# Routing one-hots laid out in pairs of tokens, so that every two-byte operand steps by one

## The reference, cut to what matters

```python
u = exp_u[ec]                                       # the picked rows
a = jax.nn.gelu(jnp.einsum('cd,chkd->chk', xc, u))
w = gc * a                                          # gc: gate of each pick
return jnp.einsum('chk,chkd->cd', w, exp_v[ec])
```

## Time and profile before

| | |
|---|---|
| median of 3 runs | 3306.38 us (3305.8 to 3314.76) |
| the profiled execution's own time | 3306.54 us |
| its span | 3304.8 us |
| TensorE's mean granted clock | 0.981 |
| DVE busy | 2340.2 us, 71% |
| PE busy | 3179.6 us, 96% |

### The profile page before, as it was taken

How to read it: one execution, slowest core, us unless ns; L and a number is a source line. 1 busy time by engine, 2 the same in 40 slices (tenths; PEclk the granted TensorE clock), 3 DMA queues, 4 the chain that set the end, 5 groups by cost and what they waited for, 6 DMA issues and landing times.

```text
span 3304.8 us, 71646 instructions
## 1 busy us (share of the span) xinstructions
PE 3179.6 (96%) x31390; PEld 2836.8 (86%) x31390; DVE 2340.2 (71%) x2685; ACT 1256.1 (38%) x1135; POOL 388.2 (12%) x284
## 2 busy tenths in 40 slices
PE   7999999999999989988989999999999999999998
PEld 4777768899999979988879998888888888888887
DVE  8596145799999877777779877578667766555554
ACT  2010143445444434333434444444443444443332
POOL 0276000000011222232212000200000000000000
PEclk8999999999999989999999999999999999999999
DMA  9657795546678988888788875556555566565553
GB/s 411 250 224 294 291 387 213 171 179 242 202 269 305 342 327 316 314 335 311 293 287 315 317 262 196 198 197 203 191 197 199 173 209 202 198 201 201 202 202 116
DMA packets 105301, 821.57 MB, mean 249 GB/s; under 512 B 12394, under 2 KB 14458, under 8 KB 15552
## 3 DMA queue, kind: packets, MB, share of 16 engines
q1 hardware_dynamic: 86112, 700.49, 58.4%
q0 software_dynamic: 16656, 115.53, 9.1%
q10 hardware_dynamic: 2304, 2.10, 0.2%
HBM read 814.00 MB, written 4.06 MB: 248 GB/s over the span
## 4 chain that ended last, share of the span: by engine, by line
PE 67%; DVE 17%; DMA 10%; issue 4%; ACT 1%; POOL 0%; ACTq 0%; DVEq 0%; SPq 0%; POOLq 0%
PE psW L587 17%; PE psW L588 17%; PE psW L589 17%; DVE ring L1191 7%; PE psW L585 7%; DMA ring<-wst_dram 4%; DMA arena<-urow_dram,rs 3%; DMA proj<-vrow_dram,rs 3%; DVE arena L1668 1%; PE psM L729 1%; PE psW L729 1%; PE psM L883 1%; PE psM L658 1%; ACT ring L2028 1%; DVE proj L1722 1%
## 5 line engine op out<-in xcount | busy, mean ns | idle before, releaser
L1191 DVE SCALAR_TENSOR_TENSOR ring<-ring 128x2048 f16<-128x2048 f32 x526 | 1200.3, 2294 | 522.8 <-ACT ring L2028 521.2
L2028 ACT ACTIVATE ring<-ring 128x2048 f16<-128x2048 f32 x526 | 1000.8, 1907 | 937.2 <-PE psW L589 776.5
L587 PE MATMUL psW<-h_act,ring 128*128 128x256 f16 (+1 forms) x5040 | 1339.7, 266 | 17.9 <-DVE ring L1191 13.0
L588 PE MATMUL psW<-h_act,ring 128*128 128x256 f16 (+1 forms) x5040 | 1338.8, 266 | 0.0
L589 PE MATMUL psW<-h_act,ring 128*128 128x256 f16 (+1 forms) x5040 | 1338.7, 266 | 0.0
L587 PE MATMUL psW<-arena,ring 128*128 128x208 f16 (+1 forms) x3072 | 800.0, 260 | 10.1 <-DVE ring L1191 5.6
L588 PE MATMUL psW<-arena,ring 128*128 128x208 f16 (+1 forms) x3072 | 799.6, 260 | 0.0
L589 PE MATMUL psW<-arena,ring 128*128 128x208 f16 (+1 forms) x3072 | 799.4, 260 | 0.0
L587 PEld LDWEIGHTS psW<-h_act,ring 128*128 128x128 f16 x5040 | 495.4, 98 | 81.1 <-issue 19.9
L589 PEld LDWEIGHTS psW<-h_act,ring 128*128 128x128 f16 x5040 | 495.6, 98 | 35.0
L588 PEld LDWEIGHTS psW<-h_act,ring 128*128 128x128 f16 x5040 | 495.6, 98 | 34.8
(11 more groups left out here) (405 smaller groups left out, 2584.7 us busy)
## 6 DMA issues: line engine op xcount, KB each, us to landing
ring<-wst_dram SPq DMA_DIRECT2D x522, 1024.0 KB
ring<-wst_dram SPq DMA_DIRECT2D x72, 2048.0 KB, 11.3
proj<-h_rows POOLq DMA_DIRECT2D x6, 1024.0 KB
x_res<-xT_dram POOLq DMA_DIRECT2D x2, 2048.0 KB, 17.5
out_dram<-x_res SPq DMA_DIRECT2D x4, 512.0 KB, 2.9
bias_rows<-proj POOLq DMA_DIRECT2D x1, 1536.0 KB, 21.8
x_res<-cmat_dram POOLq DMA_DIRECT2D x1, 1024.0 KB, 7.5
x_res<-bmat_dram ACTq DMA_DIRECT2D x8, 128.0 KB, 2.7
```

The costliest lines, as they stand in the source:

```text
L587: nc.tensor.matmul(out, whi(s, col, P), xh, start=first, stop=False)
L588: nc.tensor.matmul(out, whi(s, col, P), xl, start=False, stop=False)
L1191: ins = stt(wlo(s, c, n), ring[:, s * UNIT + c:s * UNIT + c + n], WSCALE, whi(s, c, n), ALU.mult, ALU.subtract)
L2028: act(whi(s, p2 * (UNIT // 2), UNIT // 2), ring[:, c], ACT.Copy, scale=WSCALE).then_inc(hi_done, 1)
```

## The change

The one-hots of 16 tokens were laid out token by token: the numbers of a token side by side, so the pick's number and the gate had to be repeated along the innermost dimension (step 0 there). Now two neighbouring tokens share a row of pairs: the innermost dimension has the two tokens (`x`), the number (`e`) stands outside it, and the pair of tokens (`t`) outside that. The picks and gates are then read with an inner step of one, two tokens at a time, repeated over `e`. The number table holds each number twice, so it too is read with a step of one; its one copy (L1636) writes 256 elements instead of 128, and the f16 identity moves in `dyn` to make room. PE reads each token out of the pairs: its 128 stationary and 32 moving elements now lie two elements (4 bytes) apart instead of one. The instructions, their number and order on each engine, their element counts (but for the table's copy), buffers, waits and transfers are the same.

```diff
-        ident16 = dyn[:, 320:384].bitcast(F16)
+        ident16 = dyn[:, 384:448].bitcast(F16)
...
-        iota16 = dyn[:, 256:320].bitcast(F16)
-        hot2 = [buf.bitcast(F16).rearrange("p (t e) -> p t e", t=STEP_T) for buf in (A[:, 13312:14336], J[:, 6144:7168])]
-        first1 = W[:, 1536:1792].bitcast(F16).rearrange("p (t e) -> p t e", t=STEP_T)
-        hot1 = [buf.bitcast(F16).rearrange("p (t r e) -> p t r e", t=STEP_T, r=2)
+        iota16 = dyn[:, 256:384].bitcast(F16).rearrange("p (e x) -> p e x", x=2)
+        hot2 = [buf.bitcast(F16).rearrange("p (t e x) -> p t e x", t=STEP_T // 2, x=2) for buf in (A[:, 13312:14336], J[:, 6144:7168])]
+        first1 = W[:, 1536:1792].bitcast(F16).rearrange("p (t e x) -> p t e x", t=STEP_T // 2, x=2)
+        hot1 = [buf.bitcast(F16).rearrange("p (t r e x) -> p t r e x", t=STEP_T // 2, r=2, x=2)
...
-                        mm = nc.tensor.matmul(psM[:, b, t * QUART_T:(t + 1) * QUART_T], hot2[b][:, t, :], hot1[b][:, t, r, :],
+                        mm = nc.tensor.matmul(psM[:, b, t * QUART_T:(t + 1) * QUART_T], hot2[b][:, t // 2, :, t % 2],
+                                              hot1[b][:, t // 2, r, :, t % 2],
                                               start=(r == 0), stop=(r == 1))
...
-                    D.put(v.tensor_copy(iota16, iota[:, :]))
+                    D.put(v.tensor_copy(iota16, iota[:, :].unsqueeze(2).to_broadcast([P, P, 2])))
...
-                def cols(f, w):
-                    return e16[:, f, ROWS_T + STEP_T * n:ROWS_T + STEP_T * (n + 1)].unsqueeze(2).to_broadcast([P, STEP_T, w])
+                def by_pairs(row, w):
+
+                    return row[:, ROWS_T + STEP_T * n:ROWS_T + STEP_T * (n + 1)].rearrange("p (t x) -> p t x", x=2)\
+                        .unsqueeze(2).to_broadcast([P, STEP_T // 2, w, 2])
+
+                def numbers(first, w):
+
+                    return iota16[:, first:first + w, :].unsqueeze(1).to_broadcast([P, STEP_T // 2, w, 2])
...
-                tt(first1, iota16[:, QUART_T * q:QUART_T * (q + 1)].unsqueeze(1).to_broadcast([P, STEP_T, QUART_T]),
-                   cols(0, QUART_T), ALU.is_equal).then_inc(first1_ready, 1)
-                tt(hot2[b], iota16.unsqueeze(1).to_broadcast([P, STEP_T, P]), cols(1, P), ALU.is_equal).then_inc(hot2_ready, 1)
+                tt(first1, numbers(QUART_T * q, QUART_T), by_pairs(e16[:, 0, :], QUART_T), ALU.is_equal).then_inc(first1_ready, 1)
+                tt(hot2[b], numbers(0, P), by_pairs(e16[:, 1, :], P), ALU.is_equal).then_inc(hot2_ready, 1)
...
-                    gate = g16[:, r, ROWS_T + STEP_T * n:ROWS_T + STEP_T * (n + 1)].unsqueeze(2).to_broadcast([P, STEP_T, QUART_T])
-                    ins = tt(hot1[b][:, :, r, :], first1, gate, ALU.mult)
+                    ins = tt(hot1[b][:, :, r, :, :], first1, by_pairs(g16[:, r, :], QUART_T), ALU.mult)
```

## The result

The changed kernel takes **3275.39 us** (median of 4 runs, 3272.77 to 3277.33) beside 3306.09 us for the kernel before (4 runs, 3305.48 to 3314.76): a ratio of 0.9901, with a 95% interval of 0.9883 to 0.9919. The ratio is formed from all the runs, so it isn't exactly that of the two medians (0.9907). The forecast was 3278 us. Times and ratios leave out runs in a slow state, of which there was one, in experiment 4 (4267 us at a granted clock of 0.715).

The account below looks back on a forecast made before the run. It took DVE to set the pace in u0's end and u1, and mostly a chain of transfers with DVE as a link from v0 on. 3306.5 - 15 - 13 = 3278.5, say 3278 us, range 3252 to 3294.

Parts of the forecast that it names:

- DVE's pairs: DVE's mask operations take two elements at a time, saving 1.89 us a step, 98 us of DVE's 2340 over 52 steps.
- The estimate of 1.92 us for hot2: DVE's 2048-element operation under a rule against single 4-byte words; a step would then save some 0.7 us.
- PE's strided reads: PE's loads of 128 stationary elements 4 bytes apart stay at 96 ns, so they cost 0.
- The rival at 3395 us: PE's strided stationary loads are slow, 95 ns more for each of 1664: slower, spread over 3300 to 3400 us; chance 0.13.
- u0's end and u1: Window 850 to 1022, 15 mask steps: term of 15 us, 12.4 from PE's idle time and 2.6 from the lower clock.
- so PE becomes the bound and its 13.6 us of idle time goes: End of u0 and u1: DVE's work falls from 171.6 to 143.3 us, under PE's 158.5.
- in u1 no wait of PE behind a low part over 1 us: A sign to look for in the changed kernel's profile, along with DVE below PE in u1.
- v0 to v2: 37 mask steps: dots, POOL loads and row weights come earlier; term of 13 us, bounds 0 and 56.
- 10 waits for rows or weights: v0 to v2: each PE wait for V rows or weights shortens by one step's 1.9 us, 19 us in all.
- halving the seven transfer waits: v0 to v2: 7 of 10 waits end at a transfer with DMA engines full around them, so 6.5 us was taken off.
- stay as long as now: Sign that the prediction is wrong in size: PE's waits for V rows go altogether or keep their length.
- The middle is all transfers: Rival: DVE saved, u1 gives 15 us, v0 to v2 nothing, 3291 us; counted in the forecast's own range, no separate chance.

Follow-up runs that it names:

- experiment 4: The changed kernel with each number once in the table, repeated over the two tokens by a step of zero: 3285.47 us, ratio 0.9926.
- experiment 1: The changed kernel's pair layout for PE, but DVE builds it token by token, with repeated operands, a single table and writes at a step of two: 3317.87 us.
- Experiment 7: The changed kernel with the masks of steps 0 and 1 built behind the second low part of their unit in u0's last units: 3268.85 us.
- experiment 11: The changed kernel itself, unaltered, measured a second time in a later group of runs: 3272.70 us, ratio 0.9883.
- experiment 5: The changed kernel with V row loads moved ahead of U row loads in POOL's queue where both are due in the same unit: 3237.55 us.
- 3, small ones alone: The changed kernel with only first1 and hot1 in pairs, hot2 built one element at a time into the same layout: 3293.13 us, ratio 0.9941.
- 2, hot2 alone: The changed kernel with only hot2 in pairs, the 512-element operations built one element at a time into the same layout: 3281.18 us, ratio 0.9911.
- 8, half of hot2 as well: The changed kernel with hot2 built for only 64 of the 128 numbers from step 2 on: 3276.54 us, ratio 0.9897.

## Why the prediction was right, and where it was off

**DVE's pairs: right.** 1220 and 419 ns were the lower bounds taken; 1216 and 414 to 416 were measured. The mask lines fell by 98.8 us (98 predicted). The estimate of 1.92 us for hot2, which I had worked out from the Trainium skill ("Vector Engine (DVE) Microarchitecture Reference", 5.2), did not come true: it runs at 1.216. I had stretched that section: its 1.73 ns stands for one source that hops 4 KiB at every element of a stream of 4-byte words, it lists larger figures too, and it has no row for a word that is read again. In experiments 1 to 4 the inner step decides: each operation paired exactly where all three operands step by one. No run has a step of two in the output alone, so it isn't shown that this by itself would lose the pairing.

**PE's strided reads: right.** The rival at 3395 us needed 17 ns more a load; the row says 1 ns, and experiment 1 says it without DVE's gain beside it. So a distance of 4 bytes alone doesn't explain the f32 load's 191 ns in the earlier trace rows; what does, no run here shows.

**u0's end and u1: right, with its parts off against each other.** 15 us predicted, 13.0 measured from the first mask operation to v0 (12.0 the second time). The forecast took the idle time from 13.6 to 1.2 us and 2.6 us from the lower clock; the idle time went to 4.4, and some 3.9 us came otherwise, which fits the granted clock. DVE fell below PE as forecast. The wait before the first routing step went from 2.9 to 1.1 us (the prediction's 3.1 us is another wait, behind L1740 at the end of u1, and that one went whole). The step that was mis-sized is "so PE becomes the bound and its 13.6 us of idle time goes": the stop at the next unit stayed, at 3.3 us where it was 3.6, against the sign "in u1 no wait of PE behind a low part over 1 us". Reckoned from the first mask operation, its release by DVE came 3.7 us earlier, the saving of two mask steps. But PE came 3.5 us earlier too. Windows of PE around the two stops, first of the kernel before (with columns as above: the stop, the work behind it, the work before the next stop):

```profile
857.00:860.00 3.00, 0.31 (x4) 0.07 (x1) 3.00 (x3) 1.91 (x1) 0.00 (x0) 1.00 0.00 0
860.00:866.00 6.00, 5.80 (x47) 5.28 (x48) 5.93 (x7) 0.00 (x0) 0.00 (x0) 0.72 0.77 272
866.00:871.00 5.00, 5.00 (x82) 5.00 (x80) 4.90 (x7) 2.31 (x2) 0.00 (x0) 1.00 0.24 97
```

and then of the changed one:

```profile
859.00:860.00 1.00, 0.02 (x1) 0.00 (x0) 1.00 (x2) 0.82 (x1) 0.00 (x0) 1.00 0.00 0
860.00:864.50 4.50, 4.40 (x53) 4.41 (x54) 4.47 (x5) 1.09 (x1) 0.00 (x0) 1.00 0.73 246
```

Before, a stop of 3 us was followed by 6 us at a granted clock of 0.72, which is 1.2 GHz for a bit over half of them; 47 matmuls ran. After, a stop of 1 us was followed by 1.00, and 53 matmuls ran in 4.5 us. PE regained 1.7 us there, beside the 1.8 of the shorter stop, and waited for DVE with both at the next stop. Up to the end of that stop DVE sets the pace in both kernels. Experiment 7, which takes the masks out of the way of those low parts, fits the reading: the stop shrinks to 2.5 us.

**v0 to v2: right in sign, low in size, and by another way than I worked out.** 13 us predicted, within bounds of 0 and 56; 17.9 us in the profiled execution (835.1 to 817.2 us), 27.3 in experiment 11's. The step that failed is "10 waits for rows or weights x 1.9". Waits did not each get 1.9 us shorter. The waits that DVE itself ended nearly went (15.9 to 4.3 us), while those for V rows kept most of their sum (40.2 to 38.4 us, and 33.0 in experiment 11's execution) in fewer pieces. The term also had nothing for the clock, though some 4.5 of the 17.9 us came otherwise than through idle time. That halving the seven transfer waits came close in the sum is luck.

**The sum: closer than its parts.** 3278 us stands 3 us from 3275.39. The idle time of PE gave 22.6 us in the windows of the earlier trace rows, not the 25.4 that the two terms hold; the lower clock, at 2.6 in the forecast, makes up for it (some 8 us). By the prediction's own sign its size is wrong if the waits for V rows "stay as long as now"; in the profiled execution they nearly did, and that the time came out all the same is luck as well.

**"The middle is all transfers": half right.** The transfers do hold what is left, and the DMA share there is 0.87 to 0.88. But experiment 5 moves the same bytes in another order and takes the waits away, at a share of 0.90 over the middle. So the place in POOL's queue held them, and a share of 0.87 was no proof of a limit. Nor did I see that the gain saturates. By DVE's busy time against the kernel before (2340.2 us), with the program's time against its own group's:

| | DVE, us | program, us |
|---|---|---|
| 1, distance alone | +8.8 | +8.6 |
| 4, single table | -27.8 | -23.8 |
| 3, small ones alone | -34.0 | -16.1 |
| 2, hot2 alone | -53.3 | -28.1 |
| the change | -93.8 | -30.7 and -36.7 |
| 8, half of hot2 as well | -118.5 | -33.8 |

**What stays open.** Why 4 and 3 don't stand in the order of DVE's times (the ratios have 9 and 7 us of uncertainty, and 5.2 of the 9.0 us lie ahead of the masks), what makes v1 to v2 differ by 7.5 us between executions of one kernel, and how much more than their sum pairs and order give together.

## What to carry to other kernels

A tensor-tensor operation that repeats an operand along the innermost dimension can often be turned inside out: put two neighbours innermost and the repetition outside, and double any table that would still repeat there; one operand left with an inner step of zero undoes it. Price such a saving by the idle time that its engine ends on the engine that sets the pace, with what the lower clock costs there, and not by its busy time: a third or a little more of 94 us came through here, and the next 25 us gave nothing. When a wait for a transfer outlives the saving, look at what stands ahead of it in its issuing queue before blaming the bandwidth: moving the V rows half a unit forward in a table of places gave 36 us on top of the rewrite of the masks, as much again. Without that rewrite it gave 22, since PE then waited for DVE instead.

## What the runs showed of the hardware that I had not expected

- An operand of pairs repeated by an outer step of zero, so one 4-byte word read over and over, did not keep DVE from two elements at a time: 1216 ns for 2048 elements.
- A repetition of only two elements with an inner step of zero kept the operation at one element at a time (2283 ns).
- Writing f16 with a step of two was dearer than with a step of one in such an operation that goes at one element: 2481 against 2294 ns for 2048 elements, and 725 against 695 for 512.
- A stop of PE of 1 us left the granted clock at 1.00, while one of 3 us was followed by 0.72 over 6 us, and one of 3.3 us in the changed kernel by the window below. The length of the stop doesn't settle it: behind one of 2.5 us in experiment 7 the clock was 1.00 over 10 us, and behind the same stop of 3.3 us in experiment 11 it was 0.72.

```profile
873.00:883.00 10.00, 10.00 (x117) 9.49 (x118) 10.00 (x10) 4.63 (x4) 0.00 (x0) 0.83 0.86 306
```
